# Closing layer norm in one vector step per chunk, its two-row term made by TensorE

## The reference

```python
y = jnp.concatenate([y_f, y_a], axis=-1) @ w_out[l]
x = _layernorm(DEEPNORM_ALPHA * x + gate[:, None, :] * y, ln_g[l], ln_b[l])
# _layernorm: (xf - mu) * rsqrt(var + eps) * g + b, over the 2048 features
```

## Time and profile before

| | us |
|---|---|
| median of three runs (2253.46 to 2254.05) | 2253.51 |
| the profiled execution | 2258.04 |
| its span in the trace | 2256.2 |
| PE busy | 2228.5 (99%) |
| DVE busy | 1508.0 (67%) |
| ACT busy | 1107.6 (49%) |
| POOL busy | 40.7 (2%) |
| mean granted TensorE clock | 0.994 |

### The profile page before, as it was taken

One profiled execution on the slowest core, in us unless ns is written; L12 is line 12 of the kernel. 1 busy time (PEld: TensorE's weight loads), 2 busy tenths in 40 slices (PEclk: granted clock), 3 DMA queues, 4 the chain that ended last, 5 costly groups with the idle time before them and its releaser, 6 DMA issues.

```text
span 2256.2 us, 27517 instructions
## 1 busy us (share of the span) xinstructions
PE 2228.5 (99%) x10708; PEld 1870.7 (83%) x10708; DVE 1508.0 (67%) x1883; ACT 1107.6 (49%) x1541; POOL 40.7 (2%) x66
## 2 busy tenths in 40 slices
PE   9999999999999999999999999999999999999997
PEld 7888888888888888888888888887888887888886
DVE  6665467778877777677777778766456557545556
ACT  6566455444445444444443444665465445445543
POOL 1000000000000000000000000000000000000000
PEclk9999999999999999999999999999999999999999
DMA  7534654488996988988888888472454483554473
GB/s 246 191 118 131 195 170 154 130 298 310 324 322 211 305 293 292 310 300 294 297 288 311 298 300 295 160 262 93 141 178 141 148 276 113 162 156 140 141 245 137
DMA packets 233043, 500.68 MB, mean 222 GB/s; under 512 B 15744, under 2 KB 24752, under 8 KB 231760
## 3 DMA queue, kind: packets, MB, share of 16 engines
q1 hardware_dynamic: 229440, 483.53, 64.6%
q0 software_dynamic: 3328, 14.88, 1.9%
q10 hardware_dynamic: 144, 0.51, 0.1%
HBM read 496.74 MB, written 2.12 MB: 221 GB/s over the span
## 4 chain that ended last, share of the span: by engine, by line
PE 95%; DVE 2%; ACT 1%; issue 1%; DMA 0%; POOL 0%; SPq 0%; POOLq 0%; DVEq 0%; ACTq 0%
PE bank L214 92%; PE bank L222 4%; ACT arena L231 1%; DVE arena L243 0%; DVE wl L235 0%; DMA raw<-in_w_in 0%; DVE arena L1718 0%; DVE arena L235 0%; POOL st L235 0%; ACT L231 0%; DVE hl L243 0%; ACT hh L231 0%; DVE st L252 0%; SPq L201 0%; ACT wh L231 0%
## 5 line engine op out<-in xcount | busy, mean ns | idle before, releaser
L235 DVE TENSOR_TENSOR wl<-raw,wh 128x1024 fp32r<-128x1024 f32 (+1 forms) x499 | 595.3, 1202 | 359.2 <-ACT wh L231 356.5
L231 ACT ACTIVATE wh<-raw 128x1024 fp32r<-128x1024 f32 (+1 forms) x499 | 515.3, 1043 | 485.7 <-PE bank L214 455.6
L214 PE MATMUL bank<-wh,hh 128*128 128x512 f32 (+1 forms) x1616 | 636.2, 395 | 5.1 <-DVE wl L235 2.3
L214 PE MATMUL bank<-wl,hh 128*128 128x512 f32 (+1 forms) x1616 | 625.0, 388 | 0.0
L214 PE MATMUL bank<-wh,hl 128*128 128x512 f32 (+1 forms) x1616 | 624.4, 387 | 0.0
L214 PE MATMUL bank<-wh,ah 128*128 128x512 f32 (+1 forms) x1168 | 453.2, 389 | 0.5 <-ACT ah L231 0.5
L214 PE MATMUL bank<-wh,al 128*128 128x512 f32 (+1 forms) x1168 | 450.5, 387 | 0.0
L214 PE MATMUL bank<-wl,ah 128*128 128x512 f32 (+1 forms) x1168 | 450.3, 386 | 0.0
L214 PEld LDWEIGHTS bank<-wh,hh 128*128 128x128 f32 x1616 | 304.5, 189 | 67.0 <-DVE wl L235 3.8
L214 PEld LDWEIGHTS bank<-wh,hl 128*128 128x128 f32 x1616 | 304.2, 188 | 62.4
L214 PEld LDWEIGHTS bank<-wl,hh 128*128 128x128 f32 x1616 | 305.4, 189 | 58.7
(11 more groups left out here) (116 smaller groups left out, 1279.0 us busy)
## 6 DMA issues: line engine op xcount, KB each, us to landing
raw<-in_w_in SPq DMA_DIRECT2D x256, 512.0 KB, 3.8
arena<-in_w_ada SPq DMA_DIRECT2D x107, 512.0 KB, 4.9
arena<-in_w_gate_up SPq DMA_DIRECT2D x97, 512.0 KB, 5.2
raw<-in_w_ada SPq DMA_DIRECT2D x85, 512.0 KB, 5.4
raw<-in_w_gate_up SPq DMA_DIRECT2D x79, 512.0 KB, 5.5
raw<-in_w_out SPq DMA_DIRECT2D x75, 512.0 KB, 5.4
arena<-in_w_down SPq DMA_DIRECT2D x50, 512.0 KB, 5.6
raw<-in_w_down SPq DMA_DIRECT2D x38, 512.0 KB, 5.8
```

The costliest lines, as they stand in the source:

```text
L214: return put("pe", lambda e: e.matmul(o, l, r, start=start, stop=stop_, skip_group_check=skip), w, sig, size(r) / 2400.0 * (4 if r.dtype = ...
L231: return e.activation(o, i, f, scale=scale, **k)
L235: return put(eng, lambda e: e.tensor_tensor(o, a, b, op), w, cost=vcost(eng, o))
```

## The change

The closing formula is regrouped as z·g·r + (b − mu·r·g).

- `ev_o` multiplies chunks 0 to 2 by `LG` in place as soon as their squares are taken: six more DVE operations of 128x512 per layer, each after ACT's square of the same data.
- `C2` is a pair of columns, ones and −mu·r. One small DVE operation per half makes the second column.
- For m = 1 TensorE transposes `C2` to two rows, ACT copies them to `CT`, and three matmuls with two-row operands, `CT` and `ROWS` (b over g), put b − mu·r·g of chunks 0 to 2 into three free banks. For m = 0 DVE makes that term in `XR`.
- Chunk 3 closes first, in the two old operations. Chunks 0 to 2 then need one operation for m = 1 and two for m = 0.
- The transposes that nobody reads are 8 ahead of the small transpose and 52 behind the three matmuls in layer 0 (82 before), and 36 ahead of it in layer 1 (none before).
- Two DMAs on POOL's queue load the two rows.

```diff
+            C2 = ST[:, 220:222]
+            CT = kb(9, 1)[0:2, 0:128]
+            ROWS = kb(10, 6)[0:2, :]
...
                     t2 = sq_sum(JUNK, Z[:, m, cs], SUMS[:, m, 1, n:n + 1], t1, tk["za_done"], late["jk"])
                     late["jk"] = t2
+                    t1 = tt(Z[:, m, cs], Z[:, m, cs], LG[:, cs], ALU.mult, t1, t2, late["g"])
                 y_tk[n] = [t1, t2]
...
+                dma("pool", ROWS[0:1, :], A["ln_b_2"][l:l + 1, 0:1536], "rows", [tk["za_done"]])
+                late["rows"] = dma("pool", ROWS[1:2, :], A["ln_g_2"][l:l + 1, 0:1536], "rows", [tk["za_done"]])
+                late["one"] = put("dve", lambda e: e.memset(C2[:, 0:1], 1.0), [tk["za_done"]])
...
                 t = ln_half(m, LR, t, t2, [y_tk[n] for n in range(3)])
+                tc = stt(C2[:, 1:2], MV[:, m, 0:1], -1.0, LR, ALU.mult, ALU.mult, t, late["one"])
...
-                for n in range(4):
+
+                def out_of(n, t1):
                     c2 = slice(n * 512, (n + 1) * 512)
-                    t1 = stt(Z[:, m, c2], Z[:, m, c2], MV[:, m, 0:1], LG[:, c2], ALU.subtract, ALU.mult, t, late["g"])
-                    t1 = stt_sum(XR[:, m, c2], Z[:, m, c2], LR, LB[:, c2], ALU.mult, ALU.add, SUMS[:, m, 0, n:n + 1],
-                                 t1, late["b"])
                     if l == 0:
-                        t2 = sq_sum(Z[:, m, c2], XR[:, m, c2], SUMS[:, m, 1, n:n + 1], t1)
+                        return sq_sum(Z[:, m, c2], XR[:, m, c2], SUMS[:, m, 1, n:n + 1], t1)
+                    dma("sp", od[:, m, c2], XR[:, m, c2], "out", [t1])
+
+                if m:
+                    assert len(free) == 4
+                    bks = [free.popleft() for _ in range(4)]
+                    tp = tr(BANK[bks[3]][0:2, 0:P], C2, tc, bank_rel[bks[3]], sig=True)
+                    tq = act(CT, BANK[bks[3]][0:2, 0:P], ACTF.Copy, tp)
+                    give(bks[3], tq)
+                    tb = [mm(BANK[bks[n]][:, :], CT, ROWS[:, n * 512:(n + 1) * 512], True, True, tq, late["rows"],
+                             bank_rel[bks[n]], sig=True) for n in range(3)]
+                    if l == 0:
+                        keep(52)
+                t1 = stt(Z[:, m, cs], Z[:, m, cs], MV[:, m, 0:1], LG[:, cs], ALU.subtract, ALU.mult, t, late["g"])
+                t1 = stt_sum(XR[:, m, cs], Z[:, m, cs], LR, LB[:, cs], ALU.mult, ALU.add, SUMS[:, m, 0, 3:4],
+                             t1, late["b"])
+                t2 = out_of(3, t1)
+                yield
+                for n in range(3):
+                    c2 = slice(n * 512, (n + 1) * 512)
+                    if m:
+                        row, tr_ = BANK[bks[n]][:, :], tb[n]
                     else:
-                        dma("sp", od[:, m, c2], XR[:, m, c2], "out", [t1])
+                        row = XR[:, m, c2]
+                        tr_ = stt(row, LG[:, c2], C2[:, 1:2], LB[:, c2], ALU.mult, ALU.add, tc, late["b"])
+                    t1 = stt_sum(XR[:, m, c2], Z[:, m, c2], LR, row, ALU.mult, ALU.add, SUMS[:, m, 0, n:n + 1], t, tr_)
+                    if m:
+                        give(bks[n], t1)
+                    t2 = out_of(n, t1)
                     yield
...
-            block("wo2", Y, ALL, ev_o_last, split="last", between=(lambda: (mix_now(1), keep(82))) if l == 0 else None)
+            block("wo2", Y, ALL, ev_o_last, split="last", between=lambda: (mix_now(1), keep(8)) if l == 0 else keep(36))
```

## The result

The changed kernel takes 2260.59 us (median of 20 runs, 2255.61 to 2268.71) and the kernel before 2254.11 (20 runs beside it, 2253.15 to 2259.17). The ratio is 1.0027, with a 95% interval of 1.0019 to 1.0035: slower, by 0.27%, though the lower end of the interval lies just under the 0.2% that the prediction took as the least it could tell. The forecast was 2255.3 with a range up to 2258.8, so it was wrong.

A forecast was written before the change was run, and what follows sets the result against it. PE, busy 2228.5 of 2256.2 us, was taken as the bound, with gains only where it does no useful work. Layer 0 +2.8 and layer 1 −1.0 give +1.8 on 2253.51: 2255.3 us, own range 2253.3 to 2257.5, wider range 2249.3 to 2258.8.

The forecast's parts named there:

- Closing −1.5: End of each layer: the last closing operation starts 3.7 us after r instead of 5.17, −1.5 us, at most −2.1.
- PSUM operands without surcharge: Closing operations on DVE: reading PSUM adds nothing, against the skill's fixed cycles, which would add 0.06 us each.
- The evacuation of 5.8: w_out product: with the products with g, each evacuation on DVE lasts 5.8 us instead of 2.7, +3.1.
- r 3.5 late: Layer 0, half 1: its square on ACT stands behind half 0's late square and two `wh`, so r comes 3.5 us late.
- the ring: w_out product: four-deep buffers hand delays on; unit 26 split by 1865.7, block 2's evacuation taken as 4.1 us late.
- The low clock at the row term, +1.7: Passage, layer 0: PE idles around the first 8 transposes, its clock falls, matmuls and transposes take 1.7 us more.
- The rival with the low clock at the row term: Two-row matmuls meet the low clock in both layers, 1.7 us each; layer 1 ends 1.1 late; 2257.4 us, chance 0.08.
- The clock regained at 1908, −1.9: Layer 1's first block: the 52 transposes close a PE gap, so the clock should hold, −1.9 us, bounds 0 to −1.9.
- The idle transposes: Passage, layer 0: the 52 transposes, not the norm's chain, would be late, so the start moves −0.5 us, not −1.5.
- The 4.53 us between profile and median: Whole program: runs without a profile taken as 4.53 us below the profiled execution, 2253.51 against 2258.04.
- The signs that it named: Changed profile: r near 1899.7, half 1's first DVE operation near 1895, useful transposes at 1910, last closing 3.7 after r.
- The rival "PE starves": w_out product: unit 31's buffer returns in 5.8 us, PE stands 1.1; 2258.2, or 2259.9 with more low clock; chance 0.14.

The follow-up runs named there:

- grouped: The changed kernel with both products with g of each evacuation placed behind both sums; 2255.49 us, ratio 1.0007.
- late_product2: The changed kernel with the product with g moved from `ev_o` into half 1's closing, half 0 closing as in the kernel before; 2255.79 us, ratio 0.9995.
- again: The changed kernel run once more, unedited, for a second trace; 2260.29 us, ratio 1.0024 to the kernel before.
- full_rows: The changed kernel with the operands of the row matmuls padded with zeros to 128 rows; 2258.99 us, ratio 1.001.
- grouped_short: grouped with 30 idle transposes behind the row matmuls instead of 52, operands still two rows; 2253.23 us, ratio 0.9993.
- combined: grouped and full_rows together, with 30 idle transposes behind the row matmuls instead of 52; 2250.68 us, ratio 0.9971; measured again, 2251.26 us, ratio 0.999.
- short_cover: The changed kernel with 20 idle transposes behind the row matmuls instead of 52; 2255.93 us, ratio 0.9999.
- before_bare: The kernel before without its 82 idle transposes at the passage from layer 0 to 1; 2253.38 us, ratio 0.9994.
- late_product: The changed kernel with the product with g moved from `ev_o` into the closing, giving half 0 a third operation per chunk; 2260.2 us, ratio 1.0025.
- combined_bare: combined without its 30 idle transposes behind the row matmuls; 2252.8 us, ratio 0.9995.

## Why the prediction was wrong

Its sum was +1.8 us and the traces, landmark to landmark, have +5.0. The step that failed is the one that priced TensorE's clock: a regained clock at 1908 was counted as −1.9 and is worth nothing, and the fall at the row term was priced at 1.7 for PE's gaps, while it costs 3.5 and comes with the two-row operands. Term by term:

- **Closing −1.5: right where the clock is full.** Layer 1 has 3.72 after r, forecast 3.7. The two-row matmul at 0.86 and PSUM operands without surcharge (747 ns for the closing form with a bank, 751 without) held.
- **The evacuation of 5.8: right. r 3.5 late: the mechanism right, the size not.** Measured 1.38 (0.75 in the repeat), 0.84 in layer 1 against 0.5. The products hold up DVE, DVE the half 0, half 0's last square the two `wh` and these the square of half 1, as the prediction had it; grouped and late_product2 remove exactly this. The error is in the ring: the split of unit 26 was done 1.3 earlier than 1865.7, and unit 31's high part began 3.6 after unit 27's buffer was free (1866.44 to 1870.07), the lower end of the two returns named; 4.1 had been taken.
- **The low clock at the row term, +1.7: wrong in size and in reason.** Measured 1.7 on the row matmuls and 1.8 on the idle transposes, 3.5 in all. The prediction blamed PE's gaps ahead of the matmuls. again has smaller gaps than full_rows and falls. What decides in both pairs (changed and full_rows, grouped_short and combined) is the two-row operand. The rival with the low clock at the row term had the right price per matmul, 1.7, without this reason, and put 0.08 on it; it happened in both layers in one trace, short_cover, where the three matmuls of layer 1 took 4.11. (Its price of 1.1 for layer 1 leaves out the 0.5 of late r.)
- **The clock regained at 1908, −1.9: wrong, and the largest error that nothing made up for.** In the first trace it was regained, in again it was not, and the first block takes the same time in both. The fall stood in front of matmuls that wait for ACT's and DVE's next operand in any case (0.99 for `hl` at 1915.85 in the changed kernel's trace); from the first block on, 88.9 us pass with or without it. The sum had valued a low clock by the matmuls' own lengths and not by what waited at their end.
- **The idle transposes: named as the limit, but half of it missed.** The next norm takes its input from "now" on all engines (`x_tok.extend(now())` in `pre`) and so waits for the 52 as well: after they end, the norm's first operation and its 0.9 us come on top. The low clock and this wait together make the largest loss, 3.95.
- **The 4.53 us between profile and median: wrong as a constant of profiling,** but without weight in the sum. It was the half-clock stretch at 129.7 to 139.9 us, in that execution and not in the other.

Two errors hid each other. r was forecast 2.1 too late and the low clock 1.8 too cheap, so the idle transposes end 18.3 after T0 (1905.31), where the forecast has 18.4: that agreement is luck. The 3.2 us between +1.8 and +5.0 are the 1.9 of the regained clock, 0.9 more in the passage (5.58 against 4.7), nearly all of it the norm behind the transposes, and 0.4 in layer 1. The prediction's own working with the measured sizes gives the passage: 1.4 for r, 3.5 for the clock, −0.5 for the 52 and 0.95 for the norm behind them are +5.35, against 5.58.

The signs that it named say the same. On the old scale r came at 1897.55 and not 1899.7, the first operation of half 1 on DVE at 1892.68 and not near 1895, the useful transposes at 1911.36 and not 1910. The rival "PE starves" had put 2259.9 on a time close to the measured one, but PE waits for nothing in the w_out product, so it is no better founded. The medians are 6.5 apart where the traces give 5.0; the remaining 1.5 is not resolved, given the spread of the changed kernel's runs. The prediction's chances don't agree with each other either: 0.13 below 2249.0, but 0.1 below 2249.3.

## What to carry to other kernels

Price a slower clock by the work that waits at the end of the slow stretch, not by the slow instructions. Filler on an engine is free only if nothing takes that engine's last recorded instruction as its start: look for who waits for it. And an operation put into an in-order queue behind another engine's answer costs its wait to everything behind it; grouping such operations behind independent ones gave back the 1.4 us here.

## What the runs showed of the hardware

- TensorE's granted clock fell to 1.2 GHz at or right behind the row matmuls of the passage in all seven traces where these have two-row operands, and stayed at 2.4 GHz through them in all four with 128 rows, 126 of them zeros. grouped_short and combined show it with the same gaps on PE and the same number of transposes behind. At the full clock two rows and 128 cost the same, 2.84 us for three 128x512 fp32 matmuls. These traces don't tell what in the two-row form brings it about. PE standing idle does so too: in before_bare it has nothing from 1889.4 to 1899.55, and the clock is at half from 1893.7.
- In some executions the clock is at half for 10.2 us between 128 and 140 us, in a stretch that no edit touches (before, late_product and combined_bare among these fourteen traces). T0 lies at 1891.5 to 1892.2 in these three and at 1885.8 to 1888.6 in the eleven others. It makes two levels of time 5 us apart, as much as the effect under study; single profiles can't be compared by their totals. What sets it off is not shown.
- A 128x512 operation of DVE with an operand in PSUM is no slower than one without: 682 ns for the gate product from a bank, 691 for the product from SBUF.
